# Splitting the first pair of up-projection units at k 6 in both ConvFFN layers

## The reference

```python
def conv_ffn(x, norm_g, w_up, conv_w, conv_b, w_down):
    u = rmsnorm(x, norm_g) @ w_up                       # 1024 -> 2 * 2816
    up = jnp.pad(u, ((0, 0), (CONV_WIDTH - 1, 0), (0, 0)))
    u = up[:, :-2] * conv_w[0] + up[:, 1:-1] * conv_w[1] + up[:, 2:] * conv_w[2] + conv_b
    gate, val = jnp.split(u, 2, axis=-1)
    return (jax.nn.silu(gate) * val) @ w_down           # 2816 -> 1024
```

## Time and profile before

| | |
|---|---|
| median of 3 runs | 889.96 us (887.59 to 891.66) |
| span of the profiled execution | 889.3 us |
| PE busy | 830.4 us, 93% |
| DVE busy | 632.5 us, 71% |
| ACT busy | 433.0 us, 49% |
| POOL busy | 394.5 us, 44% |
| up-projection, first matmul of layer 0 and of layer 1 | 146.81 and 670.27 us |

### The profile page before, as it was taken

The page is one execution under the profiler, slowest core; times in us unless marked ns, Lnnn a source line. Parts: engine busy times, 40 slices in busy tenths (PEclk is TensorE's granted clock), DMA queues, the critical chain, the costliest instruction groups (busy, mean ns, idle before and its releaser), DMA issues.

```text
span 889.3 us, 16860 instructions
## 1 busy us (share of the span) xinstructions
PE 830.4 (93%) x6502; PEld 802.6 (90%) x6502; DVE 632.5 (71%) x886; ACT 433.0 (49%) x555; POOL 394.5 (44%) x103
## 2 busy tenths in 40 slices
PE   8989797999989899999999999999998999898895
PEld 7889697999889899989998999999898998898894
DVE  5857868999999798446426536625648999999343
ACT  6542454646546446335435444624636555464441
POOL 3642244544554475642453442343245545544661
PEclk9989898999999999999999999999999999999898
DMA  9624324545444456773574375376334654444531
GB/s 294 193 67 138 128 83 157 188 146 186 141 152 154 150 185 210 175 243 81 155 211 104 123 188 156 101 187 197 70 111 158 205 187 143 144 166 151 165 130 47
DMA packets 135612, 137.25 MB, mean 154 GB/s; under 512 B 3521, under 2 KB 134932, under 8 KB 135572
## 3 DMA queue, kind: packets, MB, share of 16 engines
q1 hardware_dynamic: 127808, 130.03, 44.7%
q10 hardware_dynamic: 7764, 6.67, 5.6%
HBM read 135.57 MB, written 1.12 MB: 154 GB/s over the span
## 4 chain that ended last, share of the span: by engine, by line
PE 52%; DVE 20%; issue 17%; ACT 5%; DMA 3%; POOL 1%; DVEq 1%; ACTq 0%; SPq 0%; POOLq 0%
PE bank L1221 7%; PE bank L1223 7%; PE bank L1222 7%; DVE cb L1021 6%; PE banks L1221 5%; PE banks L1222 5%; PE banks L1223 5%; PE banks L1466 4%; PE bank L1435 3%; DVE ub L1013 2%; PE bank L1436 2%; PE bank L1437 2%; DVE cb L1027 2%; PE banks L1478 2%; DMA raw<-in_w_kv 2%
## 5 line engine op out<-in xcount | busy, mean ns | idle before, releaser
L413 POOL TENSOR_TENSOR wlo<-raw,whi 128x2048 fp32r<-128x2048 f32 (+1 forms) x82 | 385.6, 4707 | 454.0 <-ACT whi L451 454.0
L451 ACT ACTIVATE whi<-raw 128x2048 fp32r<-128x2048 f32 (+1 forms) x136 | 236.6, 1743 | 136.5 <-PE bank L1223 74.6
L1221 PE MATMUL bank<-xsA,whi 128*128 128x256 f32 x568 | 164.7, 290 | 13.5 <-DVE X L839 4.6
L1222 PE MATMUL bank<-xsA,whi 128*128 128x256 f32 x568 | 162.4, 286 | 0.0
L1223 PE MATMUL bank<-xsA,wlo 128*128 128x256 f32 x568 | 162.4, 286 | 0.0
L1221 PE MATMUL bank<-xsB,whi 128*128 128x256 f32 x480 | 138.4, 288 | 8.9 <-DVE ub L1013 3.9
L1223 PE MATMUL bank<-xsB,wlo 128*128 128x256 f32 x480 | 135.7, 283 | 0.0
L1222 PE MATMUL bank<-xsB,whi 128*128 128x256 f32 x480 | 135.7, 283 | 0.0
L1221 PEld LDWEIGHTS bank<-xsA,whi 128*128 128x128 f32 x568 | 110.7, 195 | 16.2 <-issue 11.6
L1021 DVE SCALAR_TENSOR_TENSOR cb<-ub,vcols,cb 128x256 f32<-128x256 f32 x88 | 119.3, 1394 | 0.2
L773 DVE TENSOR_TENSOR wlo<-raw,whi 128x2048 fp32r<-128x2048 f32 (+1 forms) x46 | 99.0, 2152 | 18.6 <-ACT whi L451 18.2
(11 more groups left out here) (211 smaller groups left out, 1722.3 us busy)
## 6 DMA issues: line engine op xcount, KB each, us to landing
raw<-in_f_w_up SPq DMA_DIRECT2D x44, 1024.0 KB, 5.1
raw<-in_w_kv SPq DMA_DIRECT2D x24, 1024.0 KB, 5.2
raw<-in_f_w_down SPq DMA_DIRECT2D x16, 1024.0 KB, 5.1
raw<-in_b_w_q SPq DMA_DIRECT2D x12, 1024.0 KB, 5.1
raw<-in_a_w_in SPq DMA_DIRECT2D x10, 1024.0 KB, 5.5
raw<-in_f_w_down SPq DMA_DIRECT2D x8, 768.0 KB, 4.8
Bi<-bias_by_distance ACTq DMA_DIRECT2D x16, 384.0 KB, 6.6
raw<-in_a_w_out SPq DMA_DIRECT2D x4, 1024.0 KB, 5.2
```

The costliest lines, as they stand in the source:

```text
L413: g.tensor_tensor(wlo[s][:, k0:KD, :], raw[s][:, k0 * CW:SLOT].rearrange("p (k c) -> p k c", c=CW), whi[s][:, k0:KD, :].bitcast(F32), ALU. ...
L451: o = a.activation(whi[s][:, k0:k1, :], raw[s][:, k0 * CW:k1 * CW] .rearrange("p (k c) -> p k c", c=CW), ACT.Copy)
L1221: t_.matmul(ps, hi_w, hi_x, start=first, stop=False)
L1222: t_.matmul(ps, hi_w, lo_x, start=False, stop=False)
```

## The change

Only TensorE's order in the first pair of each ConvFFN changes. k 0 to 5 of unit 0 are followed by k 0 to 5 of unit 1, then k 6 and 7 of unit 0, `sums`, and k 6 and 7 of unit 1. `HEAD_K` is 6. The waits go with their matmuls: unit 1's `x_new` waits now stand at its k 0, ahead of unit 0's k 6. The last use of unit 0's weights, which gives them back to ScalarE, is its k 7 as before.

```diff
                 def pair(n, p, i, step, first):
+                    if first:
+                        for g in range(2):
+                            waits = [(x_new, q0 - KD - 3 + 2 * g + c) for c in range(2)]
+                            unit(n + g, xs, FB[2 * g:2 * g + 2], wait_bank=waits, part=(0, HEAD_K),
+                                 k_wait=(lambda k: pe.wait_ge(xlo_done, x0 + k + 1))
+                                 if not g else None)
+                        for g in range(2):
+                            unit(n + g, xs, FB[2 * g:2 * g + 2], part=(HEAD_K, KD),
+                                 k_wait=(lambda k: pe.wait_ge(xlo_done, x0 + k + 1))
+                                 if not g else None)
+                            if not g:
+                                sums(s, 6, False)
+                        return
                     for g in range(2):
-                        if first:
-
-                            waits = [(x_new, q0 - KD - 3 + 2 * g + c) for c in range(2)]
-                        else:
-                            waits = [(ev_done, 4 * p + (e_up - 4 + 2 * g + c + 1)) for c in range(2)]
-                        unit(n + g, xs, FB[2 * g:2 * g + 2], i, step, wait_bank=waits,
-                             k_wait=(lambda k: pe.wait_ge(xlo_done, x0 + k + 1))
-                             if first and not g else None)
-                        if first and not g:
-                            sums(s, 6, False)
+                        waits = [(ev_done, 4 * p + (e_up - 4 + 2 * g + c + 1)) for c in range(2)]
+                        unit(n + g, xs, FB[2 * g:2 * g + 2], i, step, wait_bank=waits)
```

## The result

The changed kernel is slower: 895.98 us (893.93 to 896.7, 6 runs) against 889.71 us (887.59 to 891.66, 6 runs), ratio 1.0066 with a 95% interval of 1.0049 to 1.0084. The profiled execution has a span of 893.7 us (before 889.3) and took 895.47 us, so 1.8 us lie around the span.

What follows compares the result with a forecast made beforehand. DVE was taken to bound both ConvFFN up-projections. Layer 0's 1.9 + 2.4 + 0.3 = 4.6 us plus layer 1's 0.95 gave 5.55, added to 889.96 for 895.5 us; range 891.2 to 899.

Steps and rivals of the forecast that it cites:

- DVE bounds both stages: Both ConvFFN up-projections: DVE busy 113.17 and 112.37 of 114 us, TensorE 107.23 and 108.00, so DVE has no room.
- Layer 0, what moves: Layer 0's first pair: `sums` 4.32 us later, first bank read at 162.0, first tap at 163.35, second `wlo` ending at 171.6.
- the late start: Layer 0's first pair: DVE's first tap stands at 163.35 instead of 161.43, 1.92 us later.
- the overlap: Layer 0's first taps meet more of GpSimd's `wlo`: 2.4 us from the first, 0.3 from taps formerly on either side.
- Rival 1: DVE starts late but meets no additional GpSimd overlap: 1.9 + 0.95 = 2.85 us, 892.8 us; chance 0.25.
- The trigger: First pair: later `sums` delays rstd and bank reads; later release of unit 0's weights delays ScalarE's `whi`, then GpSimd's `wlo`.
- TensorE after the first pair: Before the second pair TensorE waits about 1.6 us for `ub` in layer 0, about 2 us for `wlo` in layer 1.
- rival 3: TensorE bounds these stages, so its removed layer 1 wait counts: 1.4 us faster, 888.6 us; chance 0.04.
- Layer 1: Layer 1's first pair: first read 1.65 us late, mostly regained by DVE's shorter `wlo`; GpSimd's next `wlo` leaves +0.95 us.
- rival 2: One more GpSimd operation meets DVE's taps: 4.64 us more, 900.1 us; chance 0.08.
- Rival 4: DVE's 1 us idle per layer and spare down-projection time swallow the delay: 890 to 891 us; chance 0.08.
- the way from the first tap to the last `hs`: In the changed profile, DVE's span over this stretch of the up-projection was to be unchanged in length.

## Why the prediction was right

The time was forecast at 895.5 and measured at 895.98, with layer 0 at +4.6 (measured 4.51) and layer 1 at +0.95 (0.82). That the total came within 0.5 us is in part luck: the stages grew by 5.33 us, the profiled span by 4.4 and the median by 6.3, and 28 runs of the kernel before lie between 887.41 and 894.58.

- **DVE bounds both stages.** Held. DVE's 113.17 us of 114 came back unchanged, and with DVE relieved TensorE had no wait left in 99 us of layer 0's stage.
- **Layer 0, what moves.** Counted from the stage's first matmul, the first read came 3.96 us later (forecast 3.84), the first tap 2.02 later (1.92), and the two `wlo` ended at 171.68 (171.6). The reads after the four taps began at 172.68 (172.7). All are within 0.15 us. `sums` itself came 4.48 us later, 4.32 forecast.
- **Layer 0, how the terms add.** The sum was right but its split wasn't. I wrote 1.9 for the late start and 2.7 for the overlap, as if one could be had without the other. With the overlap taken away the late start cost 0.57, since DVE's slack against TensorE took it up. Rival 1, which priced "no more overlap" at 1.9 in layer 0, was 1.3 too high. Shown by the kernel with `whi` ahead of the root, and only for that phase.
- **The trigger.** I named two, `sums` and the release of unit 0's weights. Each alone gives nearly the whole loss (4.33 and 4.14), because both hold back the same `whi`. They don't add either. The kernel with late sums and the `whi` ahead of the root shows that it is this `whi`, and not the root, that carries all but 0.57 us of the loss.
- **TensorE after the first pair.** Wait for the first bank read 1.39 (forecast 1.6); in layer 1 1.70 for GpSimd's `wlo` (2). Its saved 1.4 us in layer 1 did turn into a wait 1.27 longer, so rival 3 falls. The Trainium skill's rule in "Perfetto Trace Analysis", "Identifying the Most-Contended Engine", taken over the whole span, would have pointed to TensorE here; by stage it points to DVE, and 3.3% came from relieving DVE while TensorE's work stayed the same (the kernel where DVE makes the `wlo`, 860.92 us).
- **Layer 1.** First read +1.69 (1.65), DVE's own `wlo` 2.28 (2.2 to 2.3), GpSimd's next `wlo` +0.99 (0.95). This account is read from rows; no run takes layer 1's steps apart. That the layer loses nothing once DVE makes the `wlo` (-0.06) speaks for it.
- **Rivals 2 and 4.** No further GpSimd operation's worth was lost, so rival 2 falls. Rival 4 falls with the changed kernel itself: both stages grew, and TensorE's wait for the last `hs` of layer 0 stayed at 4.0 us.
- **What was wrong beside the sum.** I said that the way from the first tap to the last `hs` would keep its length. It grew by 2.5 us (138.2 to 140.7), since the additional overlap lies behind the first tap. That followed from my own sum. I said that `sums` would come 4.3 us after unit 0's k 5; 4.3 is how much later it comes. 48 matmuls lie between, 5.8 us in layer 0. The range of 891.2 to 899 takes in the forecast and rival 1 only, not the first three: rival 2 is at 900.1 and rival 3 at 888.6. And what lies around the span is 1.8 us and not 0.7, which the sum didn't use.

## What to carry to other kernels

Before moving work ahead of a small reduction such as `sums`, follow what hangs on it and what hangs on the weights' release, through ScalarE and GpSimd, to the engine that is full in that stage. A GpSimd operation that looked free was free here only where VectorE read PSUM (406 to 426 ns, always), waited, or took the reciprocal (1.75 us with and without it). And check what the reordering wants earlier as well as what it wants later: here unit 1's weights, hidden until the rest was tightened.

## What the runs showed of the hardware

- A `wlo` of 128 x 2048 takes GpSimd 4.6 us and VectorE 2.3 us when alone. On GpSimd it made two taps of VectorE, with two SBUF inputs each, take 5.24 us instead of 0.87, so it cost VectorE nearly as much as it lasts. Handing it to the slower engine was a loss: taking back four of six per three pairs made the stages 12.9 and 15.2 us shorter.
- When two `wlo` follow each other on GpSimd, VectorE gets little done in between: its two taps took 8.39 us under 9.39 us of GpSimd, and the longest single one in the kernel before 4.85. That just one got in between fits the times, and no row shows it directly. GpSimd may be held up by VectorE as well: in the kernel with `whi` ahead of the root one `wlo` beside taps of VectorE lasted 5.52 us. No run tests that.
- In the five us behind its wait of 4.6 us at the start of layer 0's up-projection TensorE had a granted clock of 0.50 to 0.53 in all nine kernels that have this wait. Behind the waits of 3.6 to 4.5 us at the start of the down-projections it was 0.50 to 0.53 in some profiles and 0.66 in others, the same kernel showing both. Behind waits of 0.67 to 2.54 us in the kernels where DVE makes the `wlo` it was 1.00.
